# One 1 MB transfer and one split instruction per engine for each weight unit, instead of two halves

## The reference, cut to what matters

```python
def swiglu(x, w1, w3, w2):
    h = jax.nn.silu(jnp.einsum("bsd,df->bsf", x, w1)) * jnp.einsum("bsd,df->bsf", x, w3)
    return jnp.einsum("bsf,fd->bsd", h, w2)

# routed layer: top-2 of 8 experts, tokens grouped by expert
def expert_block(args):
    xblk, e = args
    h = jax.nn.silu(xblk @ w1[e]) * (xblk @ w3[e])
    return h @ w2[e]
```

## Time and profile before

| | |
|---|---|
| median of 3 runs | 2317.05 us (2314.34 to 2317.45) |
| span of the profiled execution (no other time is given of it) | 2316.1 us |
| mean granted TensorE clock | 0.963 of full speed |
| TensorE / VectorE / ScalarE busy | 92% / 72% / 56% |
| read from memory | 476.94 MB |

### The profile page before, as it was taken

One profiled execution on the slowest core, in us unless ns is written; L12 is line 12 of the kernel. 1 busy time (PEld: TensorE's weight loads), 2 busy tenths in 40 slices (PEclk: granted clock), 3 DMA queues, 4 the chain that ended last, 5 costly groups with the idle time before them and its releaser, 6 DMA issues.

```text
span 2316.1 us, 38828 instructions
## 1 busy us (share of the span) xinstructions
PE 2139.2 (92%) x12823; PEld 1886.5 (81%) x12824; DVE 1659.4 (72%) x2452; ACT 1293.6 (56%) x2169; POOL 80.7 (3%) x121
## 2 busy tenths in 40 slices
PE   5989999999889866998999899999998999999992
PEld 4767888888767655997999798998997998998991
DVE  6885666666669744776777688887775888887774
ACT  4433555555444213555666577776664777776662
POOL 1001000000000011000000000000000000000002
PEclk9999999999999977999999899999999999999996
DMA  7212756566532114776777799998776999998773
GB/s 232 83 55 94 257 189 189 184 190 190 163 110 94 59 48 138 228 231 208 235 244 244 226 312 305 309 310 291 242 247 206 304 307 304 315 308 258 244 244 124
DMA packets 362763, 493.26 MB, mean 213 GB/s; under 512 B 16660, under 2 KB 317828, under 8 KB 362692
## 3 DMA queue, kind: packets, MB, share of 16 engines
q1 hardware_dynamic: 353376, 464.58, 62.5%
q0 software_dynamic: 7936, 27.03, 3.6%
q10 hardware_dynamic: 1380, 0.61, 0.1%
HBM read 476.94 MB, written 15.22 MB: 212 GB/s over the span
## 4 chain that ended last, share of the span: by engine, by line
PE 88%; issue 4%; DVE 4%; DMA 2%; ACT 1%; POOL 1%; POOLq 0%; ACTq 0%; DVEq 0%
PE PS L996 86%; PE PS L1180 1%; DVE PS L576 1%; PE PS L1013 1%; DVE OV L537 1%; DVE XN L676 0%; DMA raw<-in_expert_w 0%; DVE wlo L504 0%; DMA OV<-in_norm_mix_g 0%; ACT whi L298 0%; DVE XN L521 0%; POOL SM L851 0%; POOL l_rows L937 0%; DMA raw<-y_rows,addr 0%; DMA y_rows<-OV 0%
## 5 line engine op out<-in xcount | busy, mean ns | idle before, releaser
L996 PE MATMUL PS<-XN,whi 128*128 128x256 f32 (+3 forms) x4992 | 1392.8, 359 | 39.5 <-issue 29.6
L504 DVE TENSOR_TENSOR wlo<-raw,whi 128x1024 fp32r<-128x1024 f32 x878 | 1070.2, 1222 | 199.4 <-ACT whi L298 188.4
L996 PE MATMUL PS<-XN,wlo 128*128 128x128 f32 (+4 forms) x4672 | 1175.5, 252 | 0.0
L996 PEld LDWEIGHTS PS<-XN,whi 128*128 128x128 f32 x4992 | 948.0, 190 | 123.0 <-issue 43.7
L298 ACT ACTIVATE whi<-raw 128x1024 fp32r<-128x1024 f32 x878 | 918.7, 1050 | 58.8 <-PE PS L996 41.9
L996 PEld LDWEIGHTS PS<-XN,wlo 128*128 128x128 f32 x4672 | 898.9, 192 | 23.9
L996 PE MATMUL PS<-whi,hid 128*128 128x512 f32 (+1 forms) x1504 | 452.6, 399 | 4.3 <-DVE hid L666 4.3
L410 ACT ACTIVATE OV<-PS 128x128 f32<-128x128 f32 (+3 forms) x272 | 84.0, 309 | 440.4 <-PE PS L996 440.4
L996 PEld LDWEIGHTS PS<-whi,hid 128*128 128x128 f32 (+1 forms) x1504 | 253.9, 183 | 53.9 <-issue 4.0
L996 PE MATMUL PS<-wlo,hid 128*128 128x512 f32 (+1 forms) x864 | 271.0, 395 | 0.0
L652 DVE TENSOR_TENSOR OV<-PS,OV 128x128 f32<-128x128 f32 (+3 forms) x272 | 89.3, 328 | 209.4 <-ACT OV L410 209.4
(11 more groups left out here) (168 smaller groups left out, 718.8 us busy)
## 6 DMA issues: line engine op xcount, KB each, us to landing
raw<-in_expert_w SPq DMA_DIRECT2D x678, 512.0 KB, 4.7
raw<-in_ffn_w SPq DMA_DIRECT2D x144, 512.0 KB, 3.6
raw<-in_w_in SPq DMA_DIRECT2D x40, 512.0 KB, 4.7
raw<-in_w_out SPq DMA_DIRECT2D x16, 512.0 KB, 4.2
y_rows<-OV POOLq DMA_DIRECT2D x8, 512.0 KB, 3.0
y_rows<-OV POOLq DMA_DIRECT2D x1, 3072.0 KB, 11.7
RES<-in_x SPq DMA_DIRECT2D x4, 512.0 KB, 5.4
x_tok<-OV POOLq DMA_DIRECT2D x4, 512.0 KB, 2.9
```

The source lines that it names most:

```text
L504: dve.tensor_tensor(wlo[:, w, half(h)], raw[:, u0 % RAW, half(h)], whi[:, w, half(h)].bitcast(F32), ALU.subtract).then_inc(s["lo_done"], 1)
L996: return pe.matmul(out_, lhsT, rhs, start=start, stop=stop, skip_group_check=True)
```

## The change

A unit is brought by one transfer with one semaphore (`raw0` to `raw2`), copied by one ScalarE instruction of 2048 columns and subtracted by one VectorE instruction of 2048 columns. The function `half` goes, all counts of `lo_done` and `hi_done` are per unit. In `hidden`, `ahead` does nothing where (3i + k) is even, and splits a whole unit where it is odd. A transfer waits until the whole unit three before is subtracted.

```diff
             def load(u0, du, src, parts):
-                for h in range(2):
-                    if not (isinstance(du, int) and u0 + du < RAW):
-                        sp.wait_ge(s["lo_done"], du * 2 + (2 * (u0 - RAW) + h + 1))
-                    sp.dma_start(raw[:, u0 % RAW, half(h)].rearrange("p (a b) -> p a b", a=parts // 2),
-                                 src[:, h * parts // 2:(h + 1) * parts // 2, :]).then_inc(s[f"raw{u0 % RAW}{h}"], 16)
+                if not (isinstance(du, int) and u0 + du < RAW):
+                    sp.wait_ge(s["lo_done"], du + (u0 - RAW + 1))
+                sp.dma_start(raw[:, u0 % RAW, :].rearrange("p (a b) -> p a b", a=parts),
+                             src).then_inc(s[f"raw{u0 % RAW}"], 16)
...
-            def split(u0, du, q, halves=(0, 1)):
+            def split(u0, du, q):
                 r = u0 % RAW
-                for h in halves:
-                    act.wait_ge(s[f"raw{r}{h}"], q * 16 + 16 * (u0 // RAW + 1))
-                    act.activation(whi[:, u0 % CONV, half(h)], raw[:, r, half(h)],
-                                   ACT.Copy).then_inc(s["hi_done"], 1)
+                act.wait_ge(s[f"raw{r}"], q * 16 + 16 * (u0 // RAW + 1))
+                act.activation(whi[:, u0 % CONV, :], raw[:, r, :], ACT.Copy).then_inc(s["hi_done"], 1)
...
                     unit, h = (3 * i + k) // 2, (3 * i + k) % 2
-                    group_gate(act, unit % 3, f0 + 2 + 2 * (unit // 3), df)
-                    split(u0 + unit, du, q, (h,))
+                    if h:
+                        group_gate(act, unit % 3, f0 + 2 + 2 * (unit // 3), df)
+                        split(u0 + unit, du, q)
...
-            def split(u0, du, halves=(0, 1)):
+            def split(u0, du):
                 w = u0 % CONV
-                for h in halves:
-                    dve.wait_ge(s["hi_done"], du * 2 + (2 * u0 + h + 1))
-                    dve.tensor_tensor(wlo[:, w, half(h)], raw[:, u0 % RAW, half(h)], whi[:, w, half(h)].bitcast(F32),
-                                      ALU.subtract).then_inc(s["lo_done"], 1)
+                dve.wait_ge(s["hi_done"], du + (u0 + 1))
+                dve.tensor_tensor(wlo[:, w, :], raw[:, u0 % RAW, :], whi[:, w, :].bitcast(F32),
+                                  ALU.subtract).then_inc(s["lo_done"], 1)
...
-                        pe.wait_ge(s["lo_done"], du * 2 + 2 * (u + 1))
+                        pe.wait_ge(s["lo_done"], du + (u + 1))
```

More of the change, by code:

```diff
@@ L133, in build_program @@
         l_rows = nc.dram_tensor("l_rows", [WIN * VIS, 1], U32)
-        names = """x0 x1 x2 x3 raw00 raw01 raw10 raw11 raw20 raw21 prm_in bd_in gB0_in gB_in gF_in rw_in
+        names = """x0 x1 x2 x3 raw0 raw1 raw2 prm_in bd_in gB0_in gB_in gF_in rw_in
           const_ok bd_zero step prm_T prm_ok lam_exp sp_ok rw_hi rw_ok warm_up
@@ L157, in build_program @@
         done_at = {t: i for i, t in enumerate(Y_TILES[0] + Y_TILES[1])}
-        def half(h):
-            return slice(h * UNIT // 2, (h + 1) * UNIT // 2)
         def bank(i):
@@ L646, in ahead @@
                     unit, h = (3 * i + k) // 2, (3 * i + k) % 2
-                    group_gate(dve, unit % 3, f0 + 2 + 2 * (unit // 3), df)
-                    split(u0 + unit, du, (h,))
+                    if h:
+                        group_gate(dve, unit % 3, f0 + 2 + 2 * (unit // 3), df)
+                        split(u0 + unit, du)
                 for i in range(4):
@@ L1029, in z_waits @@
             def z_waits(l, i):
-                pe.wait_ge(s["lo_done"], 2 * (base_of[l] + i + 1))
+                pe.wait_ge(s["lo_done"], base_of[l] + i + 1)
                 if i >= 2:
@@ L1093, in mixer @@
                             pe.wait_ge(s["ylo_done"], 8 * l + pos + 1)
-                            pe.wait_ge(s["lo_done"], 2 * (base_of[l] + 10 + pos // 2 + 1))
+                            pe.wait_ge(s["lo_done"], base_of[l] + 10 + pos // 2 + 1)
                         w = (base_of[l] + 10 + pos // 2) % CONV
```

## The result

The changed kernel takes 2466.7 us (median of four runs, 2464.8 to 2470.6) against 2315.7 us for the kernel before (median of the four runs of it by then): ratio 1.065, 95% interval 1.064 to 1.067. The forecast was 2454 with a range of 2428 to 2505. The profiled execution has a span of 2464.4 us, 148.3 more than before.

A forecast was written before the change was run, and what follows sets the result against it. TensorE's matmul queue was taken as the bound, 86.4% of the chain. 2316.1 + 129 (loop) + 4 (visit ends) + 1 (dense ends) + 0.6 (start) + 2 (transfers) = 2452.7, forecast 2454 us with run median; range 2428 to 2505.

The forecast's parts named there:

- The loop of waits: 128-token visits: ScalarE-VectorE loop without TensorE takes 12.5 us against TensorE's 10.17; 2.3 us wait per group, +129 us.
- The whole instructions: Splits of 2048 columns: 2.30 us on VectorE, 1.91 on ScalarE; 66 and 83 us less busy time, buying nothing by itself.
- The gain rule: Splits: fixed latency per SBUF instruction makes one large tile beat many small ones; by that rule alone, a gain.
- 160 tokens, the draw and the ends: 160-token groups: loop 12.84 us against 12.88, taken as 0; ends of visits 0, 1, 4, 7: +1.0 each, +4.
- the rival of a lost draw: Chance 0.15: each of 13 steps costs 0.02 us more, loops 12.76 and 13.1 us at 128 and 160 tokens, about 2479.
- the mis-sized term: Ends of visits 0, 1, 4, 7: last whole split ahead of the XN subtractions, +1.0 us each, +4.
- Start and dense layer: Ahead of visit 0: first unit's whole copy +0.6 us, dense halves' ends +1, whole-unit loads at dense start +2.
- Transfers: Weight loads: 1 MB takes 6.5 us (bounds 4.8 to 9.6), hidden in the loop; exposed at dense start, +2.
- The clock: 128-token groups, chance 0.08: TensorE's waits halve its clock for half of each group, 13.6 us a group, 2515; forecast kept 1.00.

The follow-up runs named there:

- the 160-token pair: Kernel before and changed kernel, each with smallest visit window raised from 128 to 160 tokens: 2437.1 us and 2466.6 us.
- the two runs of pairs: Kernel before with both halves of a unit back to back in the changed kernel's three gaps: 2362.5 us; with subtraction also awaiting both copies: 2498.3 us.
- the run at 2375.9: Changed kernel with ScalarE's copy of a group's third unit moved behind the odd tile's c3 copy, VectorE unchanged: 2375.9 us, ratio 1.026.
- the two kernels that differ mainly in it: Changed kernel, 2466.7 us; kernel before with paired halves in its three gaps, subtraction awaiting both copies, 2498.3 us. Transfer size differs too.
- its partner: Kernel before with the smallest window of a visit raised from 128 to 160 tokens: 2437.1 us (two runs).

## Why the prediction was right, point by point

- **The loop of waits**, the step on which all rested, was right in mechanism, place and size: 12.43 us measured for 12.5, TensorE waiting for hid's low part and not for the split or a load (2.06 us in a group that TensorE began at full clock, for 2.3), and 132 us over the four visits for 129. That it does not contain TensorE is shown by the 160-token pair; that it is made of place and hand-over, by the two runs of pairs (46 us for place, 136 for the hand-over there), and that one copy's place opens or closes half of it, by the run at 2375.9.
- **The whole instructions**: 2.290 and 1.904 us measured for 2.30 and 1.91. The extrapolation from the earlier trace rows holds. So does the formula of the Trainium skill (VectorE: DVE Perf Modes, "The TRN2 errata"), 2.29. The rows of the splits on the two pages fell by 65.3 us on VectorE and 83.5 on ScalarE, for 66 and 83.
- **The gain rule** of the Trainium skill (VectorE: DVE Perf Modes, "The TRN2 errata") is true for the busy time, 41 and 61 us less on the engines' totals of the profile, and of the two kernels that differ mainly in it the one with fewer instructions is 32 us faster. The passage says nothing of the engine that waits for the result, and that decided.
- **160 tokens, the draw and the ends**: the draw was narrowly lost. The loop is 12.96 us against 12.89, 0.9 us a visit and 2.7 in all, so the rival of a lost draw was partly true. The four visits of 160 and 192 tokens, with all that follows the last, gave 10.6 us where +4 stood. The other 7.9 us lie outside the groups, 1.6 to 2.5 us a visit where +1.0 stood: that is the mis-sized term. Which step there is longer was not traced.
- **Start and dense layer**: +3.6 forecast for the time ahead of visit 0, 5.5 measured, in other places than thought. The start is not later (first projection matmul at 31.5 instead of 32.3 us, and 31.2 to 33.4 in the other runs of this study, so 0.6 could not be seen). At the start of the dense layer TensorE waits 5.20 us for hid's low part instead of 3.71; the second mixer's matmuls begin 2.1 us later, and the rest arises behind them and was not traced further.
- **Transfers**: hidden, as argued: landing in 5.1 us for 1 MB on the page, inside the 4.8 to 9.6 and below the 6.5 that I took. The mean rate in the visits is 252 GB/s for 250. Alone the transfer costs some 5 us, which no term had.
- **The clock**: I kept it at 1.00 and it was not. What it did is below. It cost little, because a stretch at half clock used up a wait that was there anyway; the price of the rival, a TensorE-bound group of 13.6 us, did not come.

## What to carry to other kernels

When one engine's output feeds another's within hand-written orders, join two instructions only after writing down the loop of waits that both orders close, and compare it with the period of the engine that bounds the stage: here 12.4 against 10.2 us, with the busy sums of both engines going down. The size of an instruction is also the size of the hand-over; if large instructions are wanted, start the producer's one place ahead of the consumer's need, and then look at what the earlier start asks for in turn (here the load). A gain or loss of this kind shows only in the stages whose bound is short enough: the same edit cost 33 us in a visit of 128 tokens and about 3 in one of 160.

## What the runs showed of the hardware

**TensorE's clock fell at some waits of 2.05 us.** The timeline of TensorE in visit 2 of the changed kernel, the down product of the even tile in two groups that follow one another:

```profile
1329.24 0.73 PE L990 MATMUL PS<-whi,hid 128*128 128x512 f32 x2 [2.06 <-DVE hid L660]
...
1341.67 0.73 PE L990 MATMUL PS<-whi,hid 128*128 128x512 f32 x2 [0.46 <-DVE hid L660]
```

The windows there, each of one group's length (busy us of PE, PEld, DVE, ACT, POOL; granted clock; DMA share; GB/s):

```profile
1330.00:1342.50 12.50, 12.04 (x78) 11.25 (x77) 8.82 (x12) 7.42 (x11) 0.00 (x0) 0.86 0.78 252
1342.50:1355.00 12.50, 10.45 (x77) 9.73 (x76) 8.81 (x12) 7.19 (x11) 0.00 (x0) 0.97 0.76 252
1355.00:1367.50 12.50, 12.02 (x79) 11.09 (x78) 8.82 (x12) 7.42 (x11) 0.00 (x0) 0.89 0.77 252
1367.50:1380.00 12.50, 10.45 (x77) 9.74 (x77) 8.82 (x12) 7.19 (x11) 0.00 (x0) 1.00 0.77 252
1380.00:1392.50 12.50, 10.44 (x77) 9.70 (x76) 8.81 (x12) 7.19 (x11) 0.00 (x0) 0.98 0.79 252
```

Behind a wait of 2.06 us the granted clock was at its lower level, 1.2 GHz, for a part of the group (0.86 in the mean), TensorE was busy 12.0 instead of 10.45 us, and its next wait was 0.46 us. I had concluded from one wait of 2.10 us that left it at 1.00 that this length is safe; it is not always. Nor does it always fall: of the five waits of 2.05 and 2.06 us between 1329 and 1417 us, four were followed by a stretch at the lower level, and the one that ended at 1378.98 was not (1.00 in windows of 2 us up to 1390). The groups of this visit stay at 12.42 us on average, so here it cost nothing: the loop was the bound.

**TensorE stands for 7.5 to 8.5 us ahead of three of the visits.** The waits of TensorE over the whole run put down to "issue" (no releaser in the profile), first in the kernel before, then in its partner with only two window sizes in the program:

```profile
PE PS L996 <- issue: 32.7, 9, 8.5
```

```profile
PE PS L996 <- issue: 11.1, 7, 4.9
```

In the kernel before TensorE stands 7.5, 8.4 and 8.5 us ahead of visits 1, 2 and 5: the three whose window is smaller than that of the visit before (160 after 192, 128 after 160, twice). In the partner no such wait is longer than 4.9 us, and ahead of its visit 1 (160 after 192 there too) it is 2.0. Its visits 0, 1 and 4 are 5.7, 11.1 and 10.2 us shorter (visit 1: 184.9 instead of 196.0 us from first c1 copy to first c1 copy). These 27.0 are most of the 33.7 us by which the partner's span came out under the expectation; the rest is that a widened visit became 36.4 us longer and not 38. Ahead of visits 4 and 7, whose window is larger than the last (160 after 128), and of visits 3 and 6, whose window is the same, TensorE waits 1.15 us, for VectorE's XN. So it is not the change as such, and not the first use of a size either, since a 128-token visit had run before visit 5. One trace of a cause is in the kernel before: the DMA queue that the profile calls "instruction" moved 2, 3 and 4 packets in the windows of these three gaps (1091 to 1099, 1286 to 1295 and 1779 to 1788 us) and none in the 9 us ahead of visits 3, 4, 6 and 7. The other 18 from 1099 to 2268 us are spread over the visits. In the partner it moved 2 packets from 1085 to 1094 us, ahead of its visit 1, and 3 in all of the 1206 us behind that. That would fit a program's code being loaded while TensorE stands, but no run was made for it, and the cause stays open.
